# Finer early refills of the weight ring, and the first expert's scatter moved between the second expert's up pieces

## The chip, the core and the metric

The kernel runs on one core of one Trainium2 chip, as one launch. The metric is the device time of the whole program in microseconds, here as the median of several executions. The engines named are TensorE (PE, with its weight loads as PEld), VectorE (DVE), ScalarE (ACT), GpSimd (POOL) and SyncE (SP). SP computes nothing in this kernel: it issues nearly all transfers from HBM, in an order written out by hand. The core's 16 DMA engines carry them out.

## The reference, cut to what matters

One layer of a hybrid encoder on 256 tokens of width 1024: a normalised input projection feeds a stick-breaking attention and a state-space branch, both are gated and projected back (`x += mixed @ w_out`), then comes a mixture of 32 experts, of which each token takes 4, and last a gated embedding. All is float32. The change touches only the mixture:

```
logits = hf @ w_router + b_router
top_val, top_idx = lax.top_k(logits, TOP_K)            # 4 of 32
gate = jax.nn.softmax(top_val, axis=-1)
# for each expert e, on the rows xb routed to it:
gu  = xb @ w_up[e] + b_up[e]                           # 1024 -> 2048
g   = jnp.minimum(gu[:, :D_FF], 7.0)
up  = jnp.clip(gu[:, D_FF:], -7.0, 7.0)
act = (up + 1.0) * g * jax.nn.sigmoid(1.702 * g)
ys  = act @ w_down[e] + b_down[e]                      # 1024 -> 1024
# out[token] += gate * ys
```

The weights of one expert are 8 MB (up) and 4 MB (down), so the 32 experts read some 400 MB from HBM.

## The kernel before, in words

**Stages.** Projection, attention, state space and output projection come first, with routing at their end. Then the 32 experts are worked off one after the other, each with its up to 64 tokens (CAP) as one block. After the last expert follow the products of the gate (`gate_product`) and the stores.

**The ring.** `ring` is a tile of SBUF with 9 places of 2 MB (PLACE = 4096 float32 in each of 128 partitions). An expert's weights are 6 pieces (n, c), each filling one place: c = 0 to 3 are the up weights (two of the eight k slices each), c = 4 and 5 the down weights (four of the eight j slices each). Piece (n, c) lies in place `spot(n, c)`, that is (6n + c) mod 9. So (0, 0) to (1, 2) fill the ring first; (1, 3) refills place 0, which held (0, 0), and in general piece (n, c) overwrites the one nine pieces ahead of it: (1, 4) that of (0, 1), (1, 5) that of (0, 2), (2, 1) and (2, 2) the down pieces (0, 4) and (0, 5), (2, 3) that of (1, 0).

**Refills.** SP issues them in order from `load_piece`. `left(n, c)` waits until PE has read the piece that is overwritten (the semaphores READ[c]; for c = 3 and 5 these are `up_u` and `y_full`). For four refills in BEHIND, (1, 3), (1, 4), (2, 1) and (2, 3), the first half (1 MB, 8 KB in each partition) is issued sooner, as soon as the semaphore `head_read` says that PE has read the first half of the old piece (line 549), and the second half after `left` (line 552). All others are issued whole after `left` (line 446, a helper; line 582 for experts 3 to 5), but (2, 0), whose second half was loaded long before (line 561). As SP works in order, a wait for one refill holds up all that come after it.

**PE's order.** For each expert: `up` (32 matmuls of 64 x 512, line 2085, in two records each; by pieces c = 0 to 3, each piece k by k, and in a k first w = 0, the left 1024 columns, and then w = 1), `gather` of the next expert's tokens (line 2049), and `down`: the turning of the activations (line 2122) and of the weights (2126), the product (2139), the bias rows of the next expert's up (`up_bias`, line 1947), and the scatter (2158): four matmuls, again of two records each, from Y into the banks SCATTER, which add one expert's output, weighted, to the tokens. The scatter waits for `wt_set` (DVE) and `y_set` (ACT's copy of the product to Y, line 951).

**DVE's order.** `expert(m, n)` at line 1496: `select` of expert n+1 (line 1336, lets `gather` go on through `sel_set`), `select_weighted` (1341), `activate` (1467, 1469, 1472, lets the turning go on through `act_set`), `gathered` (1462), `weights_back`, `pick`, and last `add_up` (1491), which adds the four scatter banks to the residual X2, each after its `sc_full`. Then the next expert's `select` begins. Y and ACTS[:, 0] lie at the same address of the arena (A_V + 2048).

Of the kernel before, what the change touches and what calls it, by code (L numbers as in the profile page):

```python
# [6 lines left out]
HALF = P // 2  # L7
# [58 lines left out]
def hybrid_layer(nc, x, p, g_mix, w_in, g_q, g_k, w_attn, a_re, a_im, log_dt, b_re, b_im, c_re, c_im, d_skip,  # L66
# [7 lines left out]
    E = w_router.shape[2]  # L74
# [11 lines left out]
    with ExitStack() as ctx:  # L86
# [187 lines left out]
        def spot(n, c):  # L274

            return (PER_EXPERT * n + c) % PLACES
# [4 lines left out]

        HALVES = {(E - 2, 3): "late_0", (E - 1, 3): "late_1", (E - 1, 5): "late_2"}
        AHEAD = {(1, 0): 0, (1, 1): 0, (1, 2): 0}
        BEHIND = {(1, 3): 1, (1, 4): 2, (2, 1): 3, (2, 3): 4}
        PARTED = {**AHEAD, **BEHIND}

        def loads():

            last, count = {}, [sum(at == i for at, _ in TURN.values()) for i in range(PLACES)]
            for n in range(E + 1):  # L290
                for c in range(PER_EXPERT if n < E else 2):
                    if not (n < E and c % 2 and together(n, c - 1)):
                        count[spot(n, c)] += 1 + ((n, c) in PARTED)
                        last[n, c] = count[spot(n, c)]
                    elif n < FIRST + PERIOD:
                        count[spot(n, c - 1)] += 1
                        last[n, c - 1] = count[spot(n, c - 1)]
            return last, count
# [128 lines left out]
        def _(sp):  # L427
# [117 lines left out]
            def load_piece(n, like, c):  # L545

                if isinstance(n, int) and (n, c) in BEHIND:
                    sp.wait_ge(S["head_read"], BEHIND[n, c])
                    sp.dma_start(place(spot(n, c))[:, 0:PLACE // 2], expert_source(n, c)[:, 0:PLACE // 2]).then_inc(
                        arrived[spot(n, c)], 16)  # L550
                    left(n, c)
                    sp.dma_start(place(spot(n, c))[:, PLACE // 2:], expert_source(n, c)[:, PLACE // 2:]).then_inc(
                        arrived[spot(n, c)], 16)
                    return
                left(n, c)
                if isinstance(n, int) and (n, c) in HALVES:
                    for h, sem in enumerate((S[HALVES[n, c]], arrived[spot(n, c)])):
                        cols = slice(h * PLACE // 2, (h + 1) * PLACE // 2)
                        sp.dma_start(place(spot(n, c))[:, cols], expert_source(n, c)[:, cols]).then_inc(sem, 16)
                elif isinstance(n, int) and (n, c) == (2, 0):  # L560
                    sp.dma_start(place(spot(n, c))[:, 0:2048], expert_source(n, c)[:, 0:2048]).then_inc(arrived[spot(n, c)], 16)
                else:
                    load_rows(spot(like, c), expert_source(n, c))
# [1074 lines left out]
        def _(pe):  # L1638
# [417 lines left out]
            def up(m, n, piece_in, beside=None, first=False):  # L2056

                if first:
                    pe.wait_ge(S["xs_half"], 1)
                else:  # L2060
                    pe.wait_ge(m["xs_set"], n + 1)
                for c in range(4):
                    if first and c == 2:
                        pe.wait_ge(m["xs_set"], n + 1)
                    halves = isinstance(n, int) and (n, c) in HALVES
                    if halves:
                        pe.wait_ge(S[HALVES[n, c]], 16)
                    piece = chunk(spot(n, c) if halves else piece_in(c), c)
                    for k in (2 * c, 2 * c + 1):
                        if halves and k == 2 * c + 1:  # L2070
                            piece_in(c)
                        if first and k == DT - 1:
                            pe.wait_ge(S["away_in"], 32)
                        if isinstance(n, int) and (n, k) == (2, 1):
                            pe.wait_ge(S["ahead_in"], 16)
                        for w in range(2):
                            for h in range(2):
                                to = bank[UG + w][HALF * h:HALF * (h + 1), :].rearrange("p (m j) -> p m j", j=4)
                                columns = piece[:, k % 2, F * w:F * (w + 1)].rearrange("p (m h j) -> p h m j", h=2, j=4)[:, h]
                                if first and k == DT - 1 and w == 0:  # L2080
                                    columns = AWAY_G.rearrange("p (m h j) -> p h m j", h=2, j=4)[:, h]
                                if first and k == DT - 1 and w == 1:
                                    to = bank[UG + w][HALF * h:HALF * (h + 1), :].rearrange("p (r m j) -> p r m j", r=2, j=4)
                                    columns = AWAY_U.rearrange("p r (m h j) -> p h r m j", h=2, j=4)[:, h]
                                last = pe.matmul(to, XS[:, k, :], columns, start=False, stop=(k == DT - 1))  # L2085
                            if k == DT - 1:
                                last.then_inc(m[("up_g", "up_u")[w]], 1)
                        if isinstance(n, int) and (n, k) in ((0, 0), (0, 2), (1, 0)):
                            last.then_inc(S["head_read"], 1)
                    if c < 3:  # L2090
                        last.then_inc(READ[c], 1)
                    if beside is not None:
                        beside(c)
# [19 lines left out]
                    if k % 2:  # L2113
                        last.then_inc(S["xt3_full"], 1)

            def down(m, n, piece_in, bias_of_next=True):

                pe.wait_ge(m["act_set"], n + 1)
                rows = ACTS[:, 1, :].rearrange("p (m j) -> p j m", j=4)
                for i, at in enumerate((ATB, UG)):  # L2120
                    for j in range(2):
                        last = pe.transpose(bank[at][:, P * j:P * (j + 1)], rows[:, 2 * i + j, :], I)  # L2122
                    last.then_inc(m["at_full"], 1)
                pe.wait_ge(m["wsel_set"], n + 1)
                for t in range(TB):
                    last = pe.transpose(bank[WTB][:, P * t:P * (t + 1)], WSEL[:, t, :], I)
                last.then_inc(m["wt_full"], 1)
                for h in range(2):
                    halves = isinstance(n, int) and (n, 4 + h) in HALVES
                    if halves:  # L2130
                        pe.wait_ge(S[HALVES[n, 4 + h]], 16)
                    piece = chunk(spot(n, 4 + h) if halves else piece_in(4 + h), 4 + h)
                    for j in range(4):
                        if h == 0 and j % 2 == 0:
                            pe.wait_ge(m["at_set"], n * 2 + j // 2 + 1)
                        if halves and j == 2:
                            piece_in(4 + h)
                        for c in range(2):
                            last = pe.matmul(bank[YB][HALF * c:HALF * (c + 1), :], ACTT[:, j, HALF * h:HALF * (h + 1)],  # L2139
                                             piece[:, j, 512 * c:512 * (c + 1)],  # L2140
                                             start=(h == 0 and j == 0), stop=(h == 1 and j == 3))
                        if isinstance(n, int) and (n, h, j) == (0, 0, 1):
                            last.then_inc(S["head_read"], 1)
                    last.then_inc(READ[4 + h], 1)
                if bias_of_next:
                    up_bias(m, n + 1)

                if isinstance(n, int) and n == E - 1:
                    turn_ahead(3)
                pe.wait_ge(m["wt_set"], n + 1)  # L2150
                pe.wait_ge(m["y_set"], n + 1)
                if isinstance(n, int) and n == E - 1:
                    scatter_turned()
                for q in range(4):
                    t, c = divmod(q, 2)
                    rows = slice(HALF * c, HALF * (c + 1))
                    at = (SCATTER_LAST if isinstance(n, int) and n == E - 1 else SCATTER)[q]
                    pe.matmul(bank[at][:, :], WSELT[rows, t, :], Y[rows, :], start=True,  # L2158
                              stop=True).then_inc(m["sc_full"], 1)

            def ring_piece(like, g=0):

# [56 lines left out]
            gather(M, 1)  # L2219
            vacant(WTB, ATB, YB, 6, 7)  # L2220
            pe.wait_ge(S["flag_set"], 1)
            down(M, 0, ring_piece(0))
            for n in range(1, FIRST):
                up(M, n, ring_piece(n))
                gather(M, n + 1)
                down(M, n, ring_piece(n))

# [114 lines left out]
```

## Time and profile before

| | us |
|---|---|
| median of 3 executions | 1152.17 (1151.75 to 1153.05) |
| the profiled execution | 1151.3 |
| its span, first to last instruction | 1149.6 |
| PE busy | 1110.7 (97%) |
| DVE, ACT, POOL busy | 385.4, 177.0, 185.6 |
| queue of SP's transfers, share of 16 engines | 91.0% |
| chain that ended last | PE 68%, DMA 30% |
| matmuls of `up` (line 2085), 2040 records | 457.2 |
| matmuls of `down` (line 2139), 1024 records | 228.5 |

The span is cut into 40 slices on the page; each shows how busy the engines were and how many GB/s the DMA engines moved. The chain is followed back from the last instruction, at each step to what released it. Of the five columns of page and rows that show a count in brackets, it is the number of instructions.

### The profile page before, as it was taken

What the parts mean: (1) busy time and instruction counts of PE and PEld (TensorE: products, weight loads), DVE (VectorE), ACT (ScalarE), POOL (GpSimd) and SP (SyncE); (2) the same over time, 40 slices, a digit from 0 to 9 for tenths busy, and PEclk for the clock granted to TensorE, in tenths of its full rate; (3) what the DMA queues carried; (4) which work ended last, traced back from release to release, by engine and by line L of the source; (5) the groups of instructions that cost most, each with busy time, mean ns of one, the idle gap of its engine ahead of it and who ended that gap; (6) DMA issues with size and microseconds to landing.
All of it is one profiled execution on the core that took longest, in us unless ns stands there. A gap on an engine that the chain in (4) does not pass through costs nothing.

```text
span 1149.6 us, 15939 instructions
## 1 busy us (share of the span) xinstructions
PE 1110.7 (97%) x6537; PEld 490.1 (43%) x6537; DVE 385.4 (34%) x844; ACT 177.0 (15%) x336; POOL 185.6 (16%) x195
## 2 busy tenths in 40 slices
PE   9999999999999999998999999999999999999998
PEld 4578886534333333333333333333333333333344
DVE  6658846522222232222232232222212122122226
ACT  2360114500000000000211111111111111010113
POOL 2988998100000000000000000000000000000005
PEclk9999999999999999999999999999999999999999
DMA  9933268899999999999999999999999999999991
GB/s 316 369 109 137 98 279 334 305 426 428 427 426 433 431 432 430 432 433 430 430 432 433 426 434 434 425 434 434 426 434 433 428 433 433 428 434 427 425 418 45
DMA packets 42930, 440.40 MB, mean 383 GB/s; under 512 B 9877, under 2 KB 10449, under 8 KB 24722
## 3 DMA queue, kind: packets, MB, share of 16 engines
q1 hardware_dynamic: 42306, 438.36, 91.0%
q0 software_dynamic: 480, 1.57, 0.4%
q8 instruction: 22, 0.36, 0.1%
q14 instruction: 10, 0.08, 0.0%
q10 hardware_dynamic: 112, 0.02, 0.0%
HBM read 438.89 MB, written 1.05 MB: 383 GB/s over the span
## 4 chain that ended last, share of the span: by engine, by line
PE 68%; DMA 30%; DVE 1%; issue 0%; ACT 0%; SPq 0%; DVEq 0%
PE bank L2085 24%; DMA ring<-in_w_up_dram 18%; PE bank L2139 14%; DMA ring<-in_w_down_dram 12%; PE bank L1697 7%; PE bank L1714 4%; PE bank L2158 4%; PE bank L2049 2%; PE bank L1862 2%; PE bank L1907 2%; PE bank L1947 2%; PE bank L2268 2%; PE bank L2122 1%; PE bank L2196 1%; PE bank L1772 0%
## 5 line engine op out<-in xcount | busy, mean ns | idle before, releaser
L2085 PE MATMUL bank<-ring,arena 128*64 128x512 f32 x2040 | 457.2, 605 | 17.8 <-DMA ring<-in_w_up_dram 17.6
L2085 PEld LDWEIGHTS bank<-ring,arena 128*64 128x64 f32 x2040 | 145.0, 139 | 324.6 <-issue 293.9
L2139 PE MATMUL bank<-ring,arena 128*64 128x512 f32 x1024 | 228.5, 599 | 10.5 <-DMA ring<-in_w_down_dram 9.6
L1491 DVE TENSOR_TENSOR arena<-arena,bank 128x512 f32<-128x512 f32 x128 | 79.4, 682 | 280.1 <-PE bank L2158 280.0
L728 POOL TENSOR_TENSOR ring<-ring 128x2048 f32<-128x2048 f32 x1 | 4.5, 4536 | 909.6 <-DMA ring<-in_w_ple_gate_dram 909.6
L1467 DVE TENSOR_SCALAR arena<-bank 128x512 f32<-128x512 f32 x32 | 22.1, 691 | 360.1 <-PE bank L2085 360.1
L2139 PEld LDWEIGHTS bank<-ring,arena 128*64 128x64 f32 x1024 | 73.5, 137 | 144.9 <-issue 137.6
L946 ACT ACTIVATE arena<-arena 128x512 f32<-128x512 f32 x32 | 20.2, 630 | 499.9 <-DVE arena L1467 499.9
L1697 PE MATMUL bank<-arena,ring 128*128 128x256 f32 x384 | 85.9, 382 | 0.0
L1697 PEld LDWEIGHTS bank<-arena,ring 128*128 128x128 f32 x384 | 72.0, 190 | 12.4 <-issue 3.1
L2158 PE MATMUL bank<-arena 64*128 64x512 f32 x256 | 63.5, 614 | 0.0
L2049 PEld LDWEIGHTS bank<-arena 128*128 128x128 bf16 x1488 | 45.1, 98 | 25.2 <-issue 25.2
L951 ACT ACTIVATE arena<-bank 128x512 f32<-128x512 f32 x32 | 19.1, 597 | 232.9 <-PE bank L2139 232.9
L2049 PE MATMUL bank<-arena 128*128 128x64 bf16 x1488 | 48.8, 193 | 0.0
L1714 PE MATMUL bank<-ring,arena 128*128 128x512 f32 x96 | 42.1, 594 | 0.0
L2158 PEld LDWEIGHTS bank<-arena 64*128 64x128 f32 x256 | 22.2, 186 | 40.2 <-issue 40.2
L1947 PE MATMUL bank<-arena 32*64 32x512 f32 x256 | 34.8, 613 | 0.0
L949 ACT ACTIVATE arena<-bank 128x256 f32<-128x256 f32 x64 | 21.1, 381 | 48.7 <-PE bank L2122 48.7
L1714 PEld LDWEIGHTS bank<-ring,arena 128*128 128x128 f32 x96 | 17.9, 190 | 21.6 <-issue 21.0
L2122 PE MATMUL bank<-ident,arena 128*128 128x128 f32 x128 | 23.9, 310 | 0.6
L946 ACT ACT_TABLE_LOAD x19 | 24.4, 1283 | 0.3
L2268 PE MATMUL bank<-ring 128*128 128x512 f32 (+1 forms) x64 | 24.3, 540 | 0.0
(292 smaller groups left out, 827.5 us busy)
## 6 DMA issues: line engine op xcount, KB each, us to landing
ring<-in_w_up_dram SPq DMA_DIRECT2D x40, 4096.0 KB, 33.2
ring<-in_w_down_dram SPq DMA_DIRECT2D x24, 4096.0 KB, 33.3
ring<-in_w_up_dram SPq DMA_DIRECT2D x38, 2048.0 KB, 25.6
ring<-in_w_down_dram SPq DMA_DIRECT2D x14, 2048.0 KB, 15.0
ring<-in_w_up_dram SPq DMA_DIRECT2D x19, 1024.0 KB, 7.7
ring<-in_w_in_dram SPq DMA_DIRECT2D x7, 2048.0 KB, 18.2
ring<-in_w_glu_dram SPq DMA_DIRECT2D x4, 1024.0 KB, 6.2
ring<-in_w_out_dram SPq DMA_DIRECT2D x2, 2048.0 KB, 8.4
```

The lines of the kernel that those rows point to most:

```text
L946: act.activation(ACTS[:, 2, :], ACTS[:, 0, :], ACT.Silu, scale=ALPHA).then_inc(m["sig_set"], 1)
L1491: dve.tensor_tensor(part, part, bank[at][:, :], ALU.add).then_inc(m["sc_add"], 1)
L1697: last = pe.matmul(b[:, SEQ * i:SEQ * (i + 1)], weight(key, a)[:, k, P * m:P * (m + 1)], rhs[:, k, :], start=(k == 0), stop=(k == n - 1))
L1714: last = pe.matmul(b[:, :], HT[:, k, t * P:(t + 1) * P], weight(("in", n), DT)[:, k, :], start=(k == 0), stop=(k == DT - 1))
L1862: last = pe.matmul(b[:, P * m:P * (m + 1)], w[:, k, P * m:P * (m + 1)], of[:, k, :], start=start and m == 0 and k == 0, stop=(k == 1), ski ...
L1947: pe.matmul(bank[UG + w][HALF * h:HALF * (h + 1), :], PICK[rows, :], BUP[rows, :], start=True, stop=False)
L2049: last = pe.matmul(bank[GX][:, CAP * d:CAP * (d + 1)], XB[t][:, part, P * d:P * (d + 1)], SELB[:, t, :], start=(i == 0), stop=(i == 3 * TB ...
L2085: last = pe.matmul(to, XS[:, k, :], columns, start=False, stop=(k == DT - 1))
L2122: last = pe.transpose(bank[at][:, P * j:P * (j + 1)], rows[:, 2 * i + j, :], I)
L2139: last = pe.matmul(bank[YB][HALF * c:HALF * (c + 1), :], ACTT[:, j, HALF * h:HALF * (h + 1)], piece[:, j, 512 * c:512 * (c + 1)], start=(h ...
L2158: pe.matmul(bank[at][:, :], WSELT[rows, t, :], Y[rows, :], start=True, stop=True).then_inc(m["sc_full"], 1)
L2268: last = pe.matmul(b, of[:, k, :], w[:, k, cols], start=start and k == 0, stop=(k == 3), skip_group_check=True)
```

## The change

Three things. **BEHIND** now lists for each refill its leading parts as (from, to, count of `head_read`). Of (1, 3) three quarters (0.5 MB each) are issued each on its own count and the last quarter after `left`; of (1, 4) two quarters and then a half; (1, 5) and (2, 2), issued whole before, come in two halves, and (2, 1) and (2, 3) as before. The counts of transfers per place (PARTED, LOAD) follow. **`head_read`** is raised at new points: for expert 0 after the w = 0 half of k = 0, 1 and 2, after (0, 4), and after j = 1 of the second down piece. **The scatter** of expert 0 no longer stands at the end of its `down`; each of its four matmuls comes after one of the four up pieces of expert 1. DVE's code is unchanged.

```diff
-        BEHIND = {(1, 3): 1, (1, 4): 2, (2, 1): 3, (2, 3): 4}
-        PARTED = {**AHEAD, **BEHIND}
+        BEHIND = {(1, 3): ((0, 1024, 1), (1024, 2048, 2), (2048, 3072, 3)), (1, 4): ((0, 1024, 4), (1024, 2048, 5)),
+                  (1, 5): ((0, 2048, 6),), (2, 1): ((0, 2048, 7),), (2, 2): ((0, 2048, 8),), (2, 3): ((0, 2048, 9),)}
+        PARTED = {**{key: 1 for key in AHEAD}, **{key: len(parts) for key, parts in BEHIND.items()}}
...
-                        count[spot(n, c)] += 1 + ((n, c) in PARTED)
+                        count[spot(n, c)] += 1 + PARTED.get((n, c), 0)
...
-                    sp.wait_ge(S["head_read"], BEHIND[n, c])
-                    sp.dma_start(place(spot(n, c))[:, 0:PLACE // 2], expert_source(n, c)[:, 0:PLACE // 2]).then_inc(
-                        arrived[spot(n, c)], 16)
+                    for lo, hi, read in BEHIND[n, c]:
+                        sp.wait_ge(S["head_read"], read)
+                        sp.dma_start(place(spot(n, c))[:, lo:hi], expert_source(n, c)[:, lo:hi]).then_inc(
+                            arrived[spot(n, c)], 16)
                     left(n, c)
-                    sp.dma_start(place(spot(n, c))[:, PLACE // 2:], expert_source(n, c)[:, PLACE // 2:]).then_inc(
+                    sp.dma_start(place(spot(n, c))[:, hi:], expert_source(n, c)[:, hi:]).then_inc(
                         arrived[spot(n, c)], 16)
...
-                        if isinstance(n, int) and (n, k) in ((0, 0), (0, 2), (1, 0)):
+                            if first and k < 3 and w == 0:
+                                last.then_inc(S["head_read"], 1)
+                        if isinstance(n, int) and (n, k) in ((0, 0), (0, 2), (0, 4), (1, 0)):
                             last.then_inc(S["head_read"], 1)
...
+            def scatter(m, n, q):
+
+                t, c = divmod(q, 2)
+                rows = slice(HALF * c, HALF * (c + 1))
+                at = (SCATTER_LAST if isinstance(n, int) and n == E - 1 else SCATTER)[q]
+                pe.matmul(bank[at][:, :], WSELT[rows, t, :], Y[rows, :], start=True,
+                          stop=True).then_inc(m["sc_full"], 1)
+
+            def scatter_of_first(q):
+
+                if q == 0:
+                    pe.wait_ge(M["wt_set"], 1)
+                    pe.wait_ge(M["y_set"], 1)
+                scatter(M, 0, q)
...
-                        if isinstance(n, int) and (n, h, j) == (0, 0, 1):
+                        if isinstance(n, int) and (n, h, j) in ((0, 0, 1), (0, 1, 1)):
                             last.then_inc(S["head_read"], 1)
...
+                if not scatter_here:
+                    return
...
-            down(M, 0, ring_piece(0))
+            down(M, 0, ring_piece(0), scatter_here=False)
             for n in range(1, FIRST):
-                up(M, n, ring_piece(n))
+                up(M, n, ring_piece(n), beside=scatter_of_first if n == 1 else None)
```

## Rows read from the trace of the kernel before

**Rows 1.** The page: what the DMA engines moved in each of 40 slices
```profile
GB/s 316 369 109 137 98 279 334 305 426 428 427 426 433 431 432 430 432 433 430 430 432 433 426 434 434 425 434 434 426 434 433 428 433 433 428 434 427 425 418 45
```

**Rows 2.** Chain that ended last, in order: start us, us, what
```profile
1072.65 35.94 DMA ring<-in_w_down_dram
...
1108.63 7.09 PE bank L2139 x32
```

**Rows 3.** Stretches: length, busy of PE, PEld, DVE, ACT, POOL; PE clock, DMA share, GB/s
```profile
25.00:55.00 30.00, 30.00 (x99) 15.59 (x98) 23.04 (x48) 7.57 (x13) 27.12 (x65) 1.00 1.02 371
218.00:220.50 2.50, 2.50 (x15) 0.98 (x12) 0.00 (x0) 0.00 (x0) 0.00 (x0) 1.00 0.77 256
...
224.50:226.50 2.00, 2.00 (x12) 0.72 (x10) 0.80 (x2) 1.23 (x2) 0.00 (x0) 1.00 0.95 262
...
240.00:300.00 60.00, 59.76 (x369) 22.56 (x366) 16.54 (x36) 4.37 (x9) 0.00 (x0) 1.00 1.01 428
300.00:1100.00 800.00, 769.26 (x4706) 283.90 (x4704) 190.27 (x399) 85.29 (x149) 0.00 (x0) 0.99 1.00 431
```

**Rows 4.** Timeline of SP's queue: start us, us, line, what it issues
```profile
218.28 0.35 SPq L549 DMA_DIRECT2D ring<-in_w_up_dram  x1
220.00 0.33 SPq L552 DMA_DIRECT2D ring<-in_w_up_dram  x1
222.59 0.33 SPq L549 DMA_DIRECT2D ring<-in_w_down_dram  x1
...
235.75 0.33 SPq L549 DMA_DIRECT2D ring<-in_w_up_dram  x1
237.47 0.33 SPq L552 DMA_DIRECT2D ring<-in_w_up_dram  x1
...
263.97 0.33 SPq L582 DMA_DIRECT2D ring<-in_w_up_dram  x1
...
273.93 0.33 SPq L582 DMA_DIRECT2D ring<-in_w_up_dram  x1
```

**Rows 5.** Us to landing of the issues at 218.28, 235.75, 237.47, 263.97, 273.93
```profile
ring<-in_w_up_dram SPq DMA_DIRECT2D x1, 1024.0 KB, 5.3
...
ring<-in_w_up_dram SPq DMA_DIRECT2D x1, 1024.0 KB, 7.0
...
ring<-in_w_up_dram SPq DMA_DIRECT2D x1, 1024.0 KB, 7.8
...
ring<-in_w_up_dram SPq DMA_DIRECT2D x1, 2048.0 KB, 10.8
...
ring<-in_w_up_dram SPq DMA_DIRECT2D x1, 2048.0 KB, 10.7
```

**Rows 6.** Timeline of PE from expert 0's scatter to expert 2's up
```profile
241.82 1.99 PE L2158 MATMUL bank<-arena 64*128 64x512 f32 x8
243.74 13.95 PE L2085 MATMUL bank<-ring,arena 128*64 128x512 f32 x64
257.63 1.57 PE L2049 MATMUL bank<-arena 128*128 128x64 bf16 x48
259.21 0.75 PE L2122 MATMUL bank<-ident,arena 128*128 128x128 f32 x4
...
270.24 13.95 PE L2085 MATMUL bank<-ring,arena 128*64 128x512 f32 x64
```

**Rows 7.** Timeline of DVE in the same stretch
```profile
242.98 2.48 DVE L1491 TENSOR_TENSOR arena<-arena,bank 128x512 f32<-128x512 f32 x4 [8.74 <-PE bank L2158]
245.38 0.41 DVE L1336 TENSOR_SCALAR arena<-arena 128x64 bf16<-128x64 f32 x2
245.70 0.60 DVE L1341 TENSOR_SCALAR arena<-arena 128x128 f32<-128x128 f32 x2
256.88 0.69 DVE L1467 TENSOR_SCALAR arena<-bank 128x512 f32<-128x512 f32 x1 [10.58 <-PE bank L2085]
...
258.46 0.69 DVE L1472 SCALAR_TENSOR_TENSOR arena<-arena 128x512 f32<-128x512 f32 x1
```

More of the change, by code:

```diff
@@ L2114, in scatter_turned, with down @@
                         last.then_inc(S["xt3_full"], 1)
-            def down(m, n, piece_in, bias_of_next=True):
+            def scatter(m, n, q):
[9 more added lines that the diff above has]
+                scatter(M, 0, q)
+            def down(m, n, piece_in, bias_of_next=True, scatter_here=True):
                 pe.wait_ge(m["act_set"], n + 1)
@@ L2154, in down @@
                 for q in range(4):
[L2155 to L2159, printed above, removed]
+                    scatter(m, n, q)
             def ring_piece(like, g=0):
```

## The prediction

> **What bounds the kernel now.** I read the page's slices first, since PE is 97% busy and looks like the limit. It is not, from the ninth slice on: there the transfers run at 425 to 434 GB/s in nearly every slice to the last but one [rows 1], and over 800 us at 431 with a share of 1.00 [rows 3], whatever PE does. The chain of waits says the same at the end: the last long piece is 35.94 us of waiting for down weights, and only when they have landed does PE do its last 7.09 us of product [rows 2]. So the end is set by the moment when the last expert's weights land, and that is the start of the stream plus all its bytes at a fixed rate. PE's own work can cost time only where it makes the stream stop, and the stream can gain only where it does not yet run at full rate.
>
> I then looked for that place by stretches, with 428 GB/s (240 to 300 us, [rows 3]) as full rate. From 218.0 to 220.5 us the engines moved 256 GB/s, which is (428 - 256) / 428 x 2.5 = 1.0 us lost. From 224.5 to 226.5 us it is 262 GB/s, 0.8 us lost. From 240 us on the rate is full. So what an edit of the refills can give back here is about 1.8 us, 0.16% of 1152. The first of the two has a plain cause: the ring is full, the transfers before it have run out, and the first refill, (1, 3), is issued at 218.28 [rows 4], after PE has read k = 0 of expert 0. The second has none that I can name. The refill (1, 4) was issued at 222.59 [rows 4], 2 us ahead of that dip.
>
> **The first refills in quarters.** The first quarter is issued after the w = 0 half of k = 0. An expert's up is 8 k in 13.95 us, 1.74 us for one k [rows 6], so half a k is 0.87 us: the issue moves from 218.28 to about 217.4. The second quarter then comes at 218.3, the third at 219.1, the last at 220.0, where the second half was [rows 4]. As a quarter takes 1.2 us to move at full rate and the issues are 0.87 apart, nothing runs dry between them. The gain is at most 0.87 us of the 1.0 us dip; at least nothing, if on the engines that finish the earlier transfers last the first refill is not waited for (the share of 0.77 in that stretch [rows 3] says that a good part of the engine time was still in use). I take 0.8, as that stretch is short of data and not of engine time alone. (1, 4) likewise begins 0.87 sooner, at 221.7. For the dip at 224.5 I take no gain, since its refill stood in the queue already; the bounds are 0 and 0.8.
>
> **The price of smaller pieces.** Rows of 4 KB have more packets than rows of 8 KB. The trace has no 4 KB weight stream, but w_in comes in rows of 2 KB at 371 GB/s with a share of 1.02 [rows 3], against 428. That is 5.65 us against 4.90 for 2 MB, 0.75 us for 64 packets on each engine in place of 8 (16 KB rows), or 0.013 us a packet. 3 MB come in quarters now (the four of (1, 3), two of (1, 4)), with 16 packets per MB and engine in place of 8: 3 x 8 x 0.013 = 0.3 us. The ends are 0 and, at the whole 371 GB/s, 1.1 us. I take 0.3, by the count of packets.
>
> *The skill.* The Trainium skill, "DMA: Bandwidth & Descriptors", Specifications, puts the least size for line rate at 512 B, by which 4 KB rows are free and the sum would be 0.3 us better. The 371 GB/s of 2 KB rows in this trace speak against that, so the measured rate stands.
>
> **Halves of (1, 5) and (2, 2), and the earlier issues.** Five more issues of 0.33 us each [rows 4] on SP, which otherwise sits in waits: nothing, as long as each is out before its semaphore for the next comes. Back to back, two transfers of 1 MB issued at 235.75 and 237.47 landed 7.0 and 7.8 us later [rows 4, 5], at 242.75 and 245.27, so 2.5 us apart, which is the full rate: splitting adds no gap while something is queued. Once the stream is full these earlier issues give nothing. They only deepen the queue.
>
> **The scatter moved.** PE gives up 1.92 us (241.82 to 243.74, [rows 6]) ahead of expert 1's up, so (2, 3), (2, 4), (2, 5) and (3, 0) are freed 1.9 to 0.5 us sooner. The stream is at full rate there, so this is worth nothing by itself. The price is behind it. The fourth scatter matmul now stands after the last up piece, and PE reaches its end at the same 257.6 as before, as the sum of the work is the same. But DVE takes `add_up` before anything of the next expert: it waits for that fourth matmul until 257.7. Then follow one add (2.48 / 4 = 0.66 with its start), select and weighted select (245.38 to 246.30, 0.92), and the three steps of the activation, which before stood one step short of done: 3 x 0.72. The sum is 261.4, against 258.46 + 0.69 = 259.15 before [rows 7]. PE's gather waits for the select until 258.8 (1.2 us) and the turning, at 259.21 before [rows 6], for the activation until 261.5. So PE is D = 2.3 us late from expert 1's down product on. Bounds: 0, if DVE's adds overlapped with nothing in the way, which their order excludes; 3.0 with hand-offs of 0.1 us between seven steps.
>
> Who waits for that? The refill issued at 263.97 (after the first down piece of expert 1) and the one at 273.93 (after the first up piece of expert 2), and all behind them on SP. They took 10.8 and 10.7 us to land [rows 4, 5], mostly in the queue. The shortest way from issue to landing when nothing is queued ahead is that of the refill at 218.28, 5.3 us for 1 MB, so 7.8 us for 2 MB. Their slack is thus 3.0 and 2.9 us, less the 0.5 us by which the stream is now ahead: 2.4 us. D = 2.3 just fits. Later experts have more, since PE needs 270.24 - 243.74 = 26.5 us for an expert [rows 6], and the stream 12.58 MB / 431 GB/s = 29.2 us. The stall then is hidden by what is queued, and beyond 2.4 it would cost its whole excess.
>
> **The sum.** -0.8 (first dip) + 0 (second) + 0.3 (packets) + 0 (PE's delay) = -0.5 us. Against the profiled execution (1151.3, span 1149.6) this is 1150.8. That execution lies 0.9 us below the median of the runs shown, 1152.17, so for the median I give 1151.7. A measurement of this kernel can tell about 0.2%, 2.3 us, from no change; the three runs alone spread over 1.3.
>
> **The rivals.**
> - *Both dips go.* If the dip at 224.5 is also a late issue, it goes too: -0.8 - 0.8 + 0.3 = -1.3, 1150.9. For it: (1, 4) comes right there. Against it: the refill was issued 1.9 us before, and the refill at 218.28 had landed whole 5.3 us after its issue [rows 5], with 2.5 us of bytes in it. The slack above also caps a gain near 0.6 unless D is under 2.3.
> - *The earlier quarter is hidden* by the transfers that still run at 218 to 220, or the change does not bring the issue forward, and only the packets are paid: +0.3, 1152.5.
> - *The other side: PE's delay empties the queue.* If the refills at 263.97 and 273.93 have no real slack, as an engine whose queue is empty loses its time even while others still work, D passes on whole: 2.3 + 0.3 = +2.6, 1154.8. It decides from the point where D is more than the slack; each 1 us beyond costs 1 us. For it: D 2.3 against 2.4 is thin. Against it: the whole D must be paid, and a mean engine has some slack in any case; half of it (+1.2) stays within 0.2%.
> - *Something worth more than 2.3 us* that I do not see: 1149.5.
> - *A fixed price per transfer.* The refill that found the queue nearly empty took 5.3 us for what moves in 2.5 [rows 5], so 2.8 us of it are not its bytes. Paid in full for each of five more transfers, that is 14 us, 1165.7. The two landings 2.5 us apart for 1 MB each leave no room for it: it is overlapped wherever something is queued. The Trainium skill, "DMA: Bandwidth & Descriptors", Anatomy of one DMA, fits a SWDGE transfer as about 2.0 us plus its bytes at 436 GB/s, by which it would be an estimated 10 us; these are issued by SP, and the trace does not agree with that rule where transfers are queued.
>
> **How the numbers follow.** The forecast 0.60, both dips 0.15, hidden 0.13, PE's delay passed on 0.07 (half of that within 0.2%), the unseen gain 0.04, the fixed price 0.01. Faster by over 0.2%: 0.04, with a little for a lucky case of both dips, 0.05. Slower: half of the delay's, the fixed price, and a little for a delay larger than reckoned, 0.05. Within 0.2%: 0.90. The range takes in the first three cases with the bounds of the packets (+1.1) and of the runs' own spread (0.65 either way), and part of the delay: 1149.9 to 1153.9.
>
> **What would show it.** Right: first issue of (1, 3) near 217.4; 218 to 220.5 us above 380 GB/s; expert 1's turning at 261 to 262 with two new gaps on PE, before the gather and before the turning; no stretch under 415 GB/s between 260 and 290; the last expert's landing about 0.5 us sooner. Wrong: the rate between 262 and 280 us falls (then D passed on), or the dip at 224.5 is gone (then it was a late issue), or the start of the experts itself has moved.

## The result, and the profile after

The changed kernel takes 1154.41 us (median of 16 executions, 1153.71 to 1155.84) against 1152.14 of the kernel before (16 executions, 1151.31 to 1153.41): ratio 1.0021, interval 1.0014 to 1.0027. It is slower by 2.3 us, and the interval leaves out 1. That is 0.5 us above the range forecast, and the other way from the forecast. Its profiled execution took 1154.54, with a span of 1152.7 against 1149.6. The start of the experts differs from profile to profile by 0 to 0.8 us, the kernel before among them; in this one it is 0.7 us late. So what follows compares durations between points within the experts, and rates, not absolute times.

The page's slices of the kernel after, to be set against [rows 1]:

```profile
GB/s 310 374 108 139 99 274 337 310 415 382 429 428 435 423 438 433 426 434 432 428 433 436 425 437 430 427 438 429 429 436 432 425 436 433 425 437 425 426 424 45
```

A slice is 28.8 us. The ninth and tenth (230 to 288 us) have 415 and 382 where they had 426 and 428. From the eleventh on they differ by up to 8 either way and by less than 1 in the mean. So whatever the change costs, it costs it within the first three experts. The stretches of after show where (columns as in [rows 3]):

```profile
218.00:220.50 2.50, 2.50 (x14) 0.66 (x10) 0.00 (x0) 0.32 (x1) 0.00 (x0) 1.00 0.91 288
220.50:224.50 4.00, 4.00 (x24) 1.78 (x24) 2.99 (x12) 1.59 (x3) 0.00 (x0) 1.00 0.94 326
224.50:226.50 2.00, 2.00 (x12) 0.61 (x10) 1.41 (x2) 0.52 (x1) 0.00 (x0) 1.00 1.02 406
226.50:230.00 3.50, 3.50 (x20) 1.18 (x18) 0.93 (x4) 2.02 (x3) 0.00 (x0) 1.00 1.03 423
...
260.00:280.00 20.00, 17.79 (x126) 7.51 (x126) 7.86 (x19) 1.89 (x4) 0.00 (x0) 1.00 0.92 377
280.00:300.00 20.00, 19.88 (x140) 8.05 (x136) 3.29 (x6) 1.76 (x4) 0.00 (x0) 1.00 1.00 415
```

Between 260 and 300 us the mean is 396 GB/s where it was 428: (428 - 396) / 428 x 40 = 3.0 us of stream lost. That is the whole loss of the kernel and more. PE's busy time in 260 to 280 is 17.79 of 20 us. Its timeline there, with DVE's and SP's:

```profile
242.54 3.65 PE L2087 MATMUL bank<-ring,arena 128*64 128x512 f32 x16
246.12 1.12 PE L2125 MATMUL bank<-arena 64*128 64x512 f32 x2
247.18 3.65 PE L2087 MATMUL bank<-ring,arena 128*64 128x512 f32 x16
...
262.27 1.57 PE L2051 MATMUL bank<-arena 128*128 128x64 bf16 x48 [1.11 <-DVE arena L1338]
264.83 0.75 PE L2141 MATMUL bank<-ident,arena 128*128 128x128 f32 x4 [0.99 <-DVE arena L1474]
```

```profile
261.19 0.69 DVE L1493 TENSOR_TENSOR arena<-arena,bank 128x512 f32<-128x512 f32 x1 [3.95 <-PE bank L2125]
261.80 0.41 DVE L1338 TENSOR_SCALAR arena<-arena 128x64 bf16<-128x64 f32 x2
...
264.08 0.69 DVE L1474 SCALAR_TENSOR_TENSOR arena<-arena 128x512 f32<-128x512 f32 x1 [0.17 <-ACT arena L948]
```

```profile
269.59 0.33 SPq L584 DMA_DIRECT2D ring<-in_w_up_dram  x1
...
279.55 0.33 SPq L584 DMA_DIRECT2D ring<-in_w_up_dram  x1
```

From the end of the bias rows to the turning of expert 1, the kernel before took 259.21 - 241.82 = 17.39 us [rows 6]. The kernel after takes 264.83 - 242.54 = 22.29. So **PE's delay D is 4.90 us**, where the forecast had 2.3. Two gaps on PE account for 1.11 + 0.99 = 2.10 of it: the gather waits for `select`, the turning for `activate`, and DVE comes to both only after the fourth `add_up` at 261.19. The other 2.80 us are PE's own work, which has grown. The refills behind it went out at 269.59 and 279.55 instead of 263.97 and 273.93 [rows 4]. From issue to landing they took

```profile
ring<-in_w_up_dram SPq DMA_DIRECT2D x1, 2048.0 KB, 7.2
...
ring<-in_w_up_dram SPq DMA_DIRECT2D x1, 2048.0 KB, 8.0
```

us instead of 10.8 and 10.7 [rows 5]. They found an empty queue, so the stream had stopped.

At the end, the last long wait for a transfer in the chain was, before (first fence) and after (second):

```profile
1011.05 33.19 DMA ring<-in_w_up_dram
```

```profile
1014.40 33.20 DMA ring<-in_w_up_dram
```

The numbers are the start of a transfer's link and its length up to the landing, and not a wait of PE alone. The link starts 3.35 us later, of which 0.7 is the late start of the experts in this profile. So of the 3.0 us lost near 270 us some 2.6 are still there after 29 experts: a stream that is full, here 431 GB/s over 800 us in both, gives next to nothing back.

### The profile page after: what moved, and what is told of

Read it like the earlier page. It is cut to its first block, busy times and chain, and to the rows that moved or that the text cites. A ratio compares the mean times of both kernels' runs of the same rounds, so it can differ in the third digit from the quotient of the medians.

```text
span 1152.7 us, 15935 instructions
## 1 busy us (share of the span) xinstructions
PE 1113.6 (97%) x6537; PEld 490.6 (43%) x6537; DVE 383.4 (33%) x844; ACT 177.1 (15%) x336; POOL 185.7 (16%) x195
## 4 chain that ended last, share of the span: by engine, by line
PE 74%; DMA 24%; DVE 1%; issue 1%; ACT 0%; SPq 0%; DVEq 0%
PE bank L2087 27%; PE bank L2158 15%; DMA ring<-in_w_up_dram 14%; DMA ring<-in_w_down_dram 9%; PE bank L1699 7%; PE bank L2125 4%; PE bank L1716 4%; PE bank L2051 2%; PE bank L1864 2%; PE bank L1949 2%; PE bank L1909 2%; PE bank L2285 2%; PE bank L2141 1%; PE bank L2213 1%; DMA ring<-in_w_in_dram 1%
## 5 line engine op out<-in xcount | busy, mean ns | idle before, releaser
L2125 PE MATMUL bank<-arena 64*128 64x512 f32 x256 | 66.0, 615 | 0.0
```

## The experiments

Each kernel was timed beside the kernel before, with 16 executions of after, 5 of e9 and 11 of each other one. D is read as above, as the time from the end of the bias rows to expert 1's turning, less 17.39.

| kernel | us | before | ratio (95%) | D, us |
|---|---|---|---|---|
| after | 1154.41 | 1152.14 | 1.0021 (1.0014 to 1.0027) | 4.90 |
| e1 refills only | 1152.58 | 1151.85 | 1.0010 (1.0001 to 1.0019) | 0.0 |
| e2 scatter only | 1154.24 | 1151.85 | 1.0022 (1.0013 to 1.0031) | 4.91 |
| e3 after, scatter whole behind the first piece | 1152.52 | 1151.85 | 1.0008 (0.9999 to 1.0017) | 0.16 |
| e4 after, scatter whole behind the last piece | 1153.46 | 1151.85 | 1.0014 (1.0005 to 1.0023) | 3.09 |
| e5 before's refills, scatter 1, 1, 2 | 1151.80 | 1152.18 | 0.9999 (0.9990 to 1.0008) | 1.70 |
| e6 before, extra gather work | 1153.14 | 1152.18 | 1.0010 (1.0001 to 1.0019) | 2.62 |
| e7 e1 with finer (2, 1) | 1151.83 | 1152.18 | 0.9995 (0.9986 to 1.0004) | 0.0 |
| e8 e7, scatter behind the first piece | 1151.69 | 1152.18 | 0.9998 (0.9989 to 1.0007) | 0.16 |
| e9 before, more extra gather work | 1156.81 | 1151.82 | 1.0047 (1.0033 to 1.0060) | 7.23 |
| e10 e7, scatter behind the third piece | 1151.38 | 1151.82 | 0.9994 (0.9985 to 1.0003) | 0.15 |

### The two halves of the change: e1 and e2

e1 keeps the new refills and leaves the scatter where it was. e2 is the other way round.

```
# e1, in the kernel after
-            down(M, 0, ring_piece(0), scatter_here=False)
+            down(M, 0, ring_piece(0))
-                up(M, n, ring_piece(n), beside=scatter_of_first if n == 1 else None)
+                up(M, n, ring_piece(n))
# e2, in the kernel after; head_read again at k = 0, 2 of expert 0, k = 0 of expert 1, j = 1 of the down
+        BEHIND = {(1, 3): ((0, 2048, 1),), (1, 4): ((0, 2048, 2),), (2, 1): ((0, 2048, 3),), (2, 3): ((0, 2048, 4),)}
```

> The finer refills alone, the scatter where it was before. Theory 'PE late' (the loss comes from PE being some 5 us late at expert 1's down product, which empties the queue of refills): without the moved scatter nothing of it is left, so 1151.5 to 1152.3 us beside about 1152.1 of the kernel before, and PE's turning of expert 1 at about 16.5 us after expert 0's scatter as before. Theory 'small transfers' (quarters and halves cost the stream more than reckoned): the loss stays, 1154.0 to 1154.6.

> The spread scatter alone, with the refills of before. Theory 'PE late': the whole loss is there, 1154.2 to 1155.0, the refill after expert 1's first down piece lands 7.2 us after its issue, that is as fast as with an empty queue, and all later landings are 2 to 3 us late. Theory 'small transfers': 1151.9 to 1152.4.

e2 alone gives the loss, 1.0022 beside 1.0021, and its stretches have the same hole as those of after:

```profile
260.00:280.00 20.00, 17.79 (x126) 7.34 (x127) 7.86 (x19) 1.89 (x4) 0.00 (x0) 1.00 0.92 375
280.00:300.00 20.00, 19.88 (x140) 8.03 (x136) 3.29 (x6) 1.89 (x4) 0.00 (x0) 1.00 1.00 415
```

e1 has 428 GB/s over 260 to 300 us, as before. So the hole there belongs to the scatter, not to the refills. The refills alone were to gain 0.5 us and did not: the ratio is 1.0010, if anything a small loss, and 0.3 us above what was expected of e1.

### Is it the place of the scatter, or its parting? e3, e4, e5

All three change one line of `scatter_of_first(c)`, which after up piece c issues the matmuls `parts`:

```
-                if q == 0: ... scatter(M, 0, q)
+                parts = [[0, 1, 2, 3], [], [], []][c]    # e3
+                parts = [[], [], [], [0, 1, 2, 3]][c]    # e4
+                parts = [[0], [1], [2, 3], []][c]        # e5, with before's refills
+                for q in parts: scatter(M, 0, q)
```

> The changed kernel, but all four scatter matmuls together after expert 1's first up piece. Theory 'PE late', in its two parts (each change between up matmuls of 128 x 64 weights and a scatter matmul of 64 x 128 weights stands 0.46 us on PE, six of them added by the spread; and DVE cannot select for expert 2 before the fourth scatter): both parts go, one change of form is added, PE is late by 0.5 us only, 1151.3 to 1152.2. Theory 'small transfers': 1154.0 to 1154.6, as the refills are those of the changed kernel.

> The changed kernel, but all four scatter matmuls together after expert 1's last up piece. Only DVE's order is left as a cost: expert 1's turning is late by 2.0 to 2.4 us against the first k of expert 0 (4.9 in the changed kernel). Theory 'PE late' with a slack of about 2.4 us in the queue: 1151.5 to 1152.5, no loss. If the loss comes with DVE's order alone: 1153.5 to 1154.6. Theory 'small transfers': 1154.0 to 1154.6.

> The refills of before; the scatter matmuls after expert 1's up pieces 0, 1 and 2 (one, one and two of them), so that DVE has added them all before the activation of expert 1. Only the time of the split on PE is left: a lone scatter matmul between up pieces took 1.06 us in the runs so far, four together 1.91, so expert 1's turning comes 1.6 to 2.1 us later than before against expert 0. With a slack of 1.5 to 2 us in the queue the landings behind it are late by 0 to 0.5 us: 1151.8 to 1152.5. If any split scatter costs the stream as much as the full spread did: 1154.2.

Four matmuls together cost the same 1.9 us wherever they stand: behind the first piece D is 0.16. Behind the last, e4, it is 3.09, and the gaps name it:

```profile
255.97 1.99 PE L2125 MATMUL bank<-arena 64*128 64x512 f32 x8
260.00 1.57 PE L2051 MATMUL bank<-arena 128*128 128x64 bf16 x48 [2.04 <-DVE arena L1338]
262.57 0.75 PE L2143 MATMUL bank<-ident,arena 128*128 128x128 f32 x4 [0.99 <-DVE arena L1474]
```

2.04 + 0.99 = 3.03 us of waiting, no work more. This is DVE's order by itself, with all four adds late. It is 0.7 us more than the 2.0 to 2.4 expected, and the kernel is slower (the interval begins at 1.0005) where the slack was to hide it. e5 has the parting without it, since its last matmul comes ahead of the last piece:

```profile
255.01 1.13 PE L2122 MATMUL bank<-arena 64*128 64x512 f32 x4
256.07 3.65 PE L2086 MATMUL bank<-ring,arena 128*64 128x512 f32 x16
259.66 1.57 PE L2050 MATMUL bank<-arena 128*128 128x64 bf16 x48
261.24 0.75 PE L2140 MATMUL bank<-ident,arena 128*128 128x128 f32 x4
```

No gap, and yet D is 1.70. A pair of scatter matmuls holds PE for 256.07 - 255.01 = 1.06 us; a single one in after for 247.18 - 246.12 = 1.06 as well; all four for 1.92 [rows 6]. So the first of a pair is paid and the second is free. Parted into four this is 4 x 1.06 - 1.92 = 2.32 us; into 1, 1 and 2 it is 3 x 1.06 - 1.92 = 1.26. The rest is in the up: in after a piece takes 246.12 - 242.54 = 3.58 us where a fourth of 13.89 (257.63 - 243.74, [rows 6]) is 3.47. Over four pieces that is 0.44, or 0.15 for each of the three breaks that the up has now; e3 and e10, with one break, have a D of 0.16 and 0.15. Together 2.76, measured 2.80 in after; for e5 1.26 + 0.44 = 1.70, measured 1.70.

The trace's single records say why. Each scatter matmul leaves two records of 0.59 to 0.69 us. In the kernel before, those of two scatter matmuls, one on rows 0 to 63 and one on rows 64 to 127, start within 7 ns of each other, and the four take four steps of 0.53, 0.43, 0.43 and 0.53 us. The pair of e5 starts within 7 ns too and takes two steps, 0.53 and 0.53. The single one in after takes the same two steps with nothing beside it. So most of the 2.32 us, an estimated 4 x 0.43 = 1.7, is the lost running side by side, and the remaining 0.6, with the 0.44 in the up, is the price of changing between the two kinds of matmul.

The weight loads of after show the two ends of such a change:

```profile
245.17 0.14 PEld L2087 LDWEIGHTS bank<-ring,arena 128*64 128x64 f32 x2 [0.28 <-issue]
246.12 0.29 PEld L2125 LDWEIGHTS bank<-arena 64*128 64x128 f32 x2 [0.81 <-issue]
247.18 0.20 PEld L2087 LDWEIGHTS bank<-ring,arena 128*64 128x64 f32 x4 [0.76 <-issue]
```

Between up matmuls a load follows 0.28 us after the one before it. At the change from weights of 128 x 64 to 64 x 128 it waits 0.81, and at the way back 0.76, for nothing but PE itself. The Trainium skill, "TensorEngine Tiling (Array Packing)", Key Properties, says that "Changing tiling mode (not just tile) drains the TensorE" and that tiles operate independently. The trace agrees with the first at each of these changes, and with the second in the records of the pairs that start 7 ns apart.

### What a delay of PE costs the stream: e6 and e9

Here the kernel before is left as it is, and only PE is held up at the same place by doing the gather of expert 2 three or five times over (the repeats overwrite each other with the same values):

```
-                for d in range(DT):
+                for d in [d for d in range(DT) for _ in range(3 if isinstance(n, int) and n == 2 else 1)]:    # e6; 5 in e9
```

> The kernel before, with the gather of expert 2's tokens done three times over on PE (the first two results are overwritten), so 3.0 us more of PE between expert 1's up and its turning, and nothing else. Theory 'PE late': the loss is the delay less the slack of 1.5 to 2 us, so +1.0 to +1.5: 1152.8 to 1153.4. If the loss comes from something in the scatter itself (its banks, its place between up pieces): 1151.9 and no change.

> The kernel before, with the gather of expert 2's tokens done five times over on PE, which the run with three showed to be 1.3 us each: 5.2 us of delay. There 2.6 us of delay made the mean landing 1.6 us later by expert 3's fourth piece. Theory 'PE late': past the slack every microsecond counts whole, so this one is 2.6 us later than that: +3.8 to +4.6, 1155.9 to 1156.8. If a delay is paid only at its start and then absorbed by the queue, 1153.1 as with three.

```profile
257.71 4.37 PE L2049 MATMUL bank<-arena 128*128 128x64 bf16 x144
261.92 0.72 PE L2122 MATMUL bank<-ident,arena 128*128 128x128 f32 x4
```

```profile
257.93 6.18 PE L2049 MATMUL bank<-arena 128*128 128x64 bf16 x206
265.76 1.15 PE L2049 MATMUL bank<-arena 128*128 128x64 bf16 x34 [1.65 <-issue]
```

D is 2.62 in e6 and 7.23 in e9 (5.2 were meant; more below). With neither scatter nor refills touched, the same hole opens. The stretch of e6, then of e9:

```profile
260.00:280.00 20.00, 19.90 (x160) 8.66 (x158) 4.54 (x11) 1.25 (x3) 0.00 (x0) 1.00 0.98 403
```

```profile
260.00:280.00 20.00, 18.24 (x241) 10.07 (x239) 4.22 (x11) 1.26 (x3) 0.00 (x0) 1.00 0.83 340
```

So a delay of PE at this place is a cause by itself. How much of it passes on is read from the landings of expert 3's pieces (mean over the 16 DMA engines, counted from PE's first up matmul of expert 0, against the kernel before). (3, 0) is the last piece that the queue still brings in time whatever PE does, (3, 3) the one issued at 273.93 in the kernel before:

| | e5 | e6 | e4 | after | e2 | e9 |
|---|---|---|---|---|---|---|
| D, us | 1.7 | 2.6 | 3.1 | 4.9 | 4.9 | 7.2 |
| (3, 0) later by, us | 0.0 | 0.0 | 0.4 | -0.1 | -0.1 | 0.5 |
| (3, 3) later by, us | 0.4 | 1.7 | 2.1 | 2.9 | 2.9 | 5.5 |

Of D 1 to 2 us are absorbed and most of the rest is passed on: from e6 to e9 D grows by 4.6 us and the lateness by 3.8. The first row of landings shows how far such numbers carry: e9 is 0.5 late there, though its (3, 0) was issued as in the kernel before. The knee is soft, as some loss is there at 1.7 already. It has a reason in the trace. Of the refill issued at 263.97 in the kernel before, the first DMA engine to finish its share did so 8.8 us after the issue and the last at 10.8 [rows 5]. With an empty queue, in after, the first takes 6.9. So the first engine had only 1.9 us of queued work in hand, and runs dry while the others still work.

e6 came out as expected of a late PE (1152.8 to 1153.4). e9 reached the top of what was expected (1156.8), but with 2 us more delay than the expectation reckoned with, so it does not show that every microsecond counts whole. e3 was 0.3 us above its 1151.3 to 1152.2, with a D of 0.16 where 0.5 was expected.

### Where the refills' gain went: e7, e8, e10

In e1 the stream was ahead by 0.5 to 0.95 us (mean landing of the 16 engines, counted from PE's first up matmul of expert 0) for every piece up to (2, 0), so the early refills do give what the forecast claimed. With (2, 1) it was 0.8 behind. Two stretches of the kernel before (first fence) and of e1 (second) show it:

```profile
218.00:230.00 12.00, 12.00 (x60) 4.25 (x58) 5.32 (x17) 4.13 (x6) 0.00 (x0) 1.00 0.95 353
...
236.00:240.00 4.00, 4.00 (x22) 1.68 (x20) 0.00 (x0) 0.00 (x0) 0.00 (x0) 1.00 1.01 428
240.00:244.00 4.00, 4.00 (x23) 1.09 (x20) 1.02 (x2) 0.60 (x1) 0.00 (x0) 1.00 1.04 438
```

```profile
218.00:230.00 12.00, 12.00 (x60) 4.24 (x58) 5.33 (x17) 4.50 (x7) 0.00 (x0) 1.00 0.99 370
...
236.00:240.00 4.00, 4.00 (x22) 1.59 (x20) 0.00 (x0) 0.00 (x0) 0.00 (x0) 1.00 0.98 317
240.00:244.00 4.00, 4.00 (x24) 1.24 (x20) 0.25 (x1) 0.60 (x1) 0.00 (x0) 1.00 0.95 348
```

Won: (370 - 353) / 428 x 12 = 0.5 us. Lost: (428 - 317) / 428 x 4 + (438 - 348) / 438 x 4 = 1.0 + 0.8 = 1.9 us. e1's profile is of an execution of 1153.96 us, 1.4 above its median, but the hole is not its alone. The traces of all kernels with the finer refills:

| | after | e1 | e3 | e4 | e7 | e8 | e10 |
|---|---|---|---|---|---|---|---|
| (2, 1) issued as before, or a quarter sooner | as before | as before | as before | as before | sooner | sooner | sooner |
| ahead at (2, 0), us | 0.8 | 0.8 | 0.8 | 0.9 | 0.5 | 1.0 | 0.8 |
| GB/s, 236 to 244 us | 376 | 333 | 354 | 345 | 420 | 408 | 418 |
| ahead at (2, 2), us | -0.1 | -0.9 | -0.5 | -0.4 | 0.3 | 0.6 | 0.6 |

The kernel before has 433 GB/s there, and the four runs with its refills (e2, e5, e6, e9) 418 to 429. The issue of (2, 1) is tied to PE's second j of expert 0's down product, so it does not come sooner when the stream does. It comes 1.7 to 1.9 us before the first engine has finished (2, 0) in the first four columns, and 2.2 to 3.0 before that in all the other runs. A refill of 2 MB on an empty queue takes its first engine 6.9 us, of which 4.9 are its bytes at 428 GB/s, so an estimated 2.0 us of what is queued is used up before a new issue moves anything. The early stream thus finds too little queued at (2, 1), stops on some engines, and loses 0.8 to 1.7 us: its whole lead and up to 0.9 more. To test that, e7 issues the first quarter of (2, 1) one j sooner:

```
-   (2, 1): ((0, 2048, 7),), (2, 2): ((0, 2048, 8),), (2, 3): ((0, 2048, 9),)}
+   (2, 1): ((0, 1024, 7), (1024, 2048, 8)), (2, 2): ((0, 2048, 9),), (2, 3): ((0, 2048, 10),)}
-   (n, h, j) in ((0, 0, 1), (0, 1, 1)):
+   (n, h, j) in ((0, 0, 0), (0, 0, 1), (0, 1, 1)):
```

> The finer refills with the scatter at its old place, and the first half of the refill (2, 1) in two quarters, the first issued 0.87 us sooner, after j = 0 of expert 0's down product. In the run with the finer refills alone the stream was 0.8 us ahead (mean of the 16 landings against the first issue) up to the half of (2, 0) and 0.85 us behind after (2, 1). Theory 'the queue runs dry at (2, 1) because the stream is ahead there': most of both is gone, 1150.9 to 1151.7. Theory 'small transfers cost by themselves': still behind, 1152.4 to 1152.8.

> The same, with all four scatter matmuls after expert 1's first up piece (+0.15 us on PE in the run that had this). The refills (2, 3) to (3, 0) come up to 1.9 us sooner, which is worth nothing while the queue is full: the same as the run beside it within 0.3 us, 1150.9 to 1151.7 by the first theory, 1152.4 to 1152.8 by the second.

> The finer refills with (2, 1) in quarters, and all four scatter matmuls after expert 1's third up piece: the refills (2, 3), (2, 4) and (2, 5) are then 1.9 us sooner, (3, 0) 0.15 later, and DVE has added them before expert 1's activation. In the run with the scatter after the first piece the stream was 0.98 us ahead at (2, 0) and lost 0.35 of it at (2, 4), whose issue was 0.15 late. Theory 'the queue runs dry': that loss goes, the stream stays 0.6 to 0.9 us ahead: 1151.0 to 1151.5, the fastest so far. If the gain at the start is only noise: 1151.8 to 1152.2.

```profile
236.00:240.00 4.00, 4.00 (x22) 1.67 (x20) 0.00 (x0) 0.00 (x0) 0.00 (x0) 1.00 1.00 413
240.00:244.00 4.00, 4.00 (x24) 1.14 (x22) 0.96 (x2) 0.60 (x1) 0.00 (x0) 1.00 1.03 427
```

The hole is gone in e7 (413 and 427 GB/s), and in e8 and e10 with the same refills. e7's ratio is 0.9995 where e1's was 1.0010; the intervals overlap, so the times alone are only consistent with it, and the rates and landings carry the verdict. e8 and e10 move the scatter whole behind the first or the third piece, where it has no late DVE and no parting. In e10 it is

```profile
252.97 1.99 PE L2125 MATMUL bank<-arena 64*128 64x512 f32 x8
...
260.06 0.75 PE L2143 MATMUL bank<-ident,arena 128*128 128x128 f32 x4
```

and D is 0.15. e10 has the lowest ratio of all, 0.9994, some 3 us under after's, but its interval reaches 1.0003: it is not told apart from the kernel before.

## Why the prediction was wrong

**What bounds the kernel** held up: the weight stream sets the time, PE can cost only where it makes the stream stop, and what was lost at 270 us, 3.0, is for the most part, 2.6, still lost at 1047 us. One reading was too simple. The 35.94 us of [rows 2] are a transfer from its issue to its landing, and not a wait of PE, which waits only 0.16 us for the last weights at 1108.63. For the last three experts PE is nearly level with the stream, and in after it waits for no weights of an expert behind the link that ends at 1047.60.

**PE's delay (2.3 predicted, 4.90 measured)** is the first step that failed. The waits for DVE were forecast at 2.3 us, with gaps of 1.2 and about 1.1, and are 1.11 and 0.99; both are at the two steps where they were said to be. What failed is the clause "PE reaches its end at the same 257.6 as before, as the sum of the work is the same". The sum of the instructions is the same, the sum of the time is not: parted, the four scatter matmuls take 2.3 us more, and the up around them 0.4 more. In after the up and the scatter in it end at 261.1, or 260.4 counted from the same start of the experts, and not at 257.6. The upper bound of 3.0 did not hold it either, as it bounded only the hand-offs. A hint stood in [rows 6]: the eight records of the four scatter matmuls, of 0.6 us each, take 1.99 us together, so some must run side by side, and the trace's single records show which. The term called for a bound well above nothing and had none. The same error is in "(2, 3), (2, 4), (2, 5) and (3, 0) are freed 1.9 to 0.5 us sooner": counted from the start of the experts the first two went out 1.9 and 0.7 us sooner, the others 0.5 and 1.7 later. The queue hid that, as (3, 0) still landed in time.

**The slack (2.4 predicted, 1 to 2 measured, with a soft edge)** is the second step that failed, "D = 2.3 just fits", the 0 for PE's delay in the sum. It was taken from whole transfers, that is from the last engine's landing. The first engine to run dry decides when loss begins, and it had 1.9 us. e5, with a D of 1.70, lost 0.4 us in the stream and e6, with 2.62, lost 1.7, so the predicted D of 2.3 would by itself have cost an estimated 1.2 us. With D at 4.90 the loss is 2.9, where 0 was predicted.

**The rival that came true** is the other side, "PE's delay empties the queue", given 0.07 and 1154.8. Its mechanism, place (the refills after 263.97) and time were right; its own sum, a D of 2.3 without any slack, was not. It was a D of 4.9 less a slack of about 2, so that 1154.8 came near by two errors that cancel. The chance was too low for another reason: the text itself called 2.3 against 2.4 thin, with a price of 1 us for each us beyond, and then gave it 0.07.

**The refills (-0.8 + 0.3 predicted)**. The issue did come 0.85 sooner relative to the start of the experts: 218.15 in a profile whose experts are 0.7 late. The gain was there, 0.5 to 1.0 us at (2, 0) in all seven traces with the finer refills, though 218 to 220.5 us shows 288 GB/s, not the 380 forecast. The step that failed is "They only deepen the queue", said of the earlier issues behind. At (2, 1) there is no earlier issue, and the lead turned into a hole. By themselves the refills came to +0.7 us (e1, interval 0.1 to 2.2) and not to -0.5. They do not add to the scatter's loss, as e2 alone is at 1.0022. In after's own trace the hole took only the lead: the stream was level with the kernel before at (2, 2) and at (3, 0), and lost there what it lost in e2. Why the hole is 0.8 us in after and 1.7 in e1, whose code is the same up to there, stays open.

**The price of smaller pieces (0.3 predicted)** held up nearly as reckoned. By the trace's packet records the median packet of 4 KB takes 159 ns, that of 8 KB 309 and that of 2 KB 88, alike in all seven traces with the finer refills. Two of 4 KB are thus 9 ns dearer than one of 8 KB, where 13 a packet were predicted, and 24 more packets on each engine come to an estimated 0.2 us.

**The second dip (0 predicted)** was hardly a thing to forecast. With windows moved to the start of the experts, the stretch that had 262 GB/s in the kernel before has 324 to 385 in e2, e5, e6 and e9, whose refills are the same, and 338 to 410 in the seven with the finer ones. The first dip varies as much: 125 to 311 with the old refills, 256 among them, and 247 to 379 with the new. So the budget of 1.8 us was read from one execution of a stretch that differs by as much between executions. What makes it differ stays open, as does the cause of the 0 to 0.8 us in the start of the experts.

## What to carry to other kernels

Matmuls that share a shape can be worth more together than apart: before parting a group, find what one of it costs alone, with what ran beside it and both changes of shape included, and move it whole, to a place where the engine that consumes it has nothing more urgent queued behind it. Where a stream of transfers is the bound, a wait may be moved by as much as the first engine has in its queue, not the last, and most of anything beyond is lost for good. An earlier issue helps only as far as the next one whose time is set by something else, so the whole series has to move or the lead is lost at the first that doesn't. A dip read from one trace is a budget only when a second trace of the same kernel shows it too.

## What the runs showed of the hardware that was not expected

- A single 64 x 512 scatter matmul between matmuls of another weight shape costs 1.06 us, a pair on the two halves of the rows also 1.06, two pairs 1.92. The records of a pair start 7 ns apart.
- A stream 0.8 to 0.9 us ahead of the kernel before, with the next issue at its old time, lost 0.8 to 1.7 us by the end of the piece after that one, at 333 to 376 GB/s over 8 us (after, e1, e3, e4); in e1 it was 1.9 by the rates.
- The median weight packet takes 159 ns at 4 KB, 309 at 8 KB and 613 at 16 KB, in every trace read for it; the means are longer where the queue is shallow, 176 to 188 ns at 4 KB.
- In e9, PE stands still for 1.65 us in the middle of 240 equal matmuls that wait for nothing in the profile ("issue"); e6 with 144 has no such gap. It is most of what makes D 7.23 where 5.2 were meant, and the granted clock is 1.00 throughout. Its cause stays open.
